# Sparse attention of a prompt: score masks added by VectorE, fewer score matmuls, three transpose banks; the kept-row copies moved to the first feed-forward

## What is computed

```
def masked_softmax(s, mask):
    s = jnp.where(mask, s, -jnp.inf)
    m = jnp.max(s, axis=-1, keepdims=True)
    m = jnp.where(jnp.isfinite(m), m, 0.0)
    p = jnp.exp(s - m)
    return p / jnp.maximum(jnp.sum(p, axis=-1, keepdims=True), 1e-30)
...
    p_cmp = masked_softmax(ein('bqhgd,bnhd->bqhgn', q, kc) * scale, mc)
    o_cmp = ein('bqhgn,bnhd->bqhgd', p_cmp, vc)
...
    o_sel = ein('bqhgk,bqhkd->bqhgd', masked_softmax(ein('bqhgd,bqhkd->bqhgk', q_rot, ks) * scale, ms), vs)
...
    o_win = ein('bqhgn,bnhd->bqhgd', masked_softmax(ein('bqhgd,bnhd->bqhgn', q_rot, kw) * scale, mw), vw)
    o = gates[..., 0:1] * o_cmp + gates[..., 1:2] * o_sel + gates[..., 2:3] * o_win
```

## Time and profile before

| | us |
|---|---|
| median of 3 runs | 5331.67 (5325.77 to 5340.48) |
| the profiled execution, its own time | 5327.34 |
| its span on the core | 5325.6 |
| PE busy in the span | 3931.5 (74%) |
| DVE, ACT, POOL busy | 1657.2, 977.1, 1442.9 |
| `ffn0`, first to last matmul tile | about 1795 to 2570 |
| `c_in`, first matmul to the last copy | 2635 to 2852 |
| prompt attention, loads included | about 3338 to 4100 |

### The profile page before, as it was taken

How to read it: one execution, slowest core, us unless ns; L and a number is a source line. 1 busy time by engine, 2 the same in 40 slices (tenths; PEclk the granted TensorE clock), 3 DMA queues, 4 the chain that set the end, 5 groups by cost and what they waited for, 6 DMA issues and landing times. The chain is left out here.

```text
span 5325.6 us, 63783 instructions
## 1 busy us (share of the span) xinstructions
PE 3931.5 (74%) x23500; PEld 3473.1 (65%) x23500; DVE 1657.2 (31%) x3084; ACT 977.1 (18%) x2173; POOL 1442.9 (27%) x1031
## 2 busy tenths in 40 slices
PE   3999044544533899999692567799997558999998
PEld 3999033434522899999682557456654228999998
DVE  3000422223425322223203121346664232322322
ACT  1000023310112201001100011345543122100102
POOL 3332400000001533333523000134443015333333
PEclk7999555555655999999796676689999669999999
DMA  3221521151134111111287311310100321111111
GB/s 110 101 86 60 179 84 55 48 210 49 59 95 135 38 44 47 45 44 42 83 298 239 71 56 39 61 25 13 25 1 21 102 82 40 44 48 44 42 50 53
DMA packets 364821, 395.59 MB, mean 74 GB/s; under 512 B 82945, under 2 KB 330467, under 8 KB 361111
## 3 DMA queue, kind: packets, MB, share of 16 engines
q1 hardware_dynamic: 321274, 263.06, 16.3%
q10 hardware_dynamic: 32076, 82.57, 4.8%
q0 software_dynamic: 11248, 46.95, 2.5%
HBM read 326.48 MB, written 133.75 MB: 86 GB/s over the span
## 5 line engine op out<-in xcount | busy, mean ns | idle before, releaser
L550 PE MATMUL ffn_ps<-ffn_x_hi,ffn_w_hi 128*128 128x384 f32 (+1 forms) x2112 | 688.0, 326 | 17.2 <-DVE ffn_x_lo L223 17.2
L550 PE MATMUL ffn_ps<-ffn_x_lo,ffn_w_hi 128*128 128x384 f32 (+1 forms) x2112 | 684.6, 324 | 0.0
L550 PE MATMUL ffn_ps<-ffn_x_hi,ffn_w_lo 128*128 128x384 f32 (+1 forms) x2112 | 683.5, 324 | 0.0
L2266 POOL TENSOR_TENSOR nsa_p_p<-nsa_p_p,nsa_p_w 128x63 f32<-128x63 f32 (+8 forms) x384 | 299.4, 807 | 863.7 <-DVE nsa_p_w L2222 852.4
L395 POOL TENSOR_TENSOR ffn_w_hi<-ffn_w,ffn_zero 128x1024 fp32r<-128x1024 f32 (+2 forms) x152 | 254.0, 1671 | 911.6 <-PE ffn_ps L550 903.5
L550 PEld LDWEIGHTS ffn_ps<-ffn_x_hi,ffn_w_hi 128*128 128x128 f32 x2112 | 398.9, 189 | 19.6 <-issue 19.6
L550 PEld LDWEIGHTS ffn_ps<-ffn_x_hi,ffn_w_lo 128*128 128x128 f32 x2112 | 399.0, 189 | 0.0
L550 PEld LDWEIGHTS ffn_ps<-ffn_x_lo,ffn_w_hi 128*128 128x128 f32 x2112 | 398.9, 189 | 0.0
L550 PE MATMUL ffn_ps<-ffn_h_hi,ffn_w_hi 128*128 128x384 f32 (+1 forms) x1056 | 344.1, 326 | 16.8 <-DVEq L618 16.8
L550 PE MATMUL ffn_ps<-ffn_h_lo,ffn_w_hi 128*128 128x384 f32 (+1 forms) x1056 | 342.7, 324 | 0.0
L550 PE MATMUL ffn_ps<-ffn_h_hi,ffn_w_lo 128*128 128x384 f32 (+1 forms) x1056 | 342.6, 324 | 0.0
(11 more groups left out here) (520 smaller groups left out, 7407.1 us busy)
## 6 DMA issues: line engine op xcount, KB each, us to landing
out<-in_cache_a_kv ACTq DMA_DIRECT2D x8, 4088.0 KB
ffn_w<-in_w_ffn_gate SPq DMA_DIRECT2D x44, 512.0 KB, 3.9
ffn_w<-in_w_ffn_up SPq DMA_DIRECT2D x44, 512.0 KB, 3.9
z_ab<-ab_in_o SPq DMA_DIRECT2D x90, 218.0 KB, 2.0
ab_in_w<-in_w_in_ab POOLq DMA_DIRECT2D x10, 1744.0 KB, 8.3
dil_s_kv<-in_cache_a_kv SPq DMA_DIRECT2D x16, 1024.0 KB, 33.5
cmp_pg<-in_cache_c_cmp_kv SPq DMA_DIRECT2D x128, 128.0 KB, 2.0
nsa_s_kv<-in_cache_c_sel_kv SPq DMA_DIRECT2D x128, 128.0 KB, 2.1
```

Of the source, the lines that this page charges most:

```text
L550: last = nc.tensor.matmul(bank(q)[:, 0:n], x[:, slot, k], y[:, k, c:c + n], start=(k == 0 and m == 0), stop=(k == kc - 1 and m == 2))
L2266: g.tensor_tensor(row[:, at:at + c], row[:, at:at + c], w[:, m, br:br + 1].to_broadcast([P, c]), ALU.mult)
```

## The change

In the prompt attention: the masks are no longer multiplied into the bank. PE writes the scores in one matmul per half (plus the compressed one), and DVE adds the masks in place, in the bank, ahead of the maxima, with a drain between. psP has three banks, one of them gained by dropping psF: `finish` now writes into the ring of psP. ACT copies two of three turned banks, DVE the third. Rounds are taken in pairs of groups: at an even group those of the next odd group too. The constants for the mask matmuls go. And `keep_rows` leaves the input projection: ACT of the first feed-forward starts two copies at each of the steps f = 0 to 15, between the tanhs and the copies of h.

```diff
-    rounds = lambda u, g: range(lead(u, g - 1) if g else (lead(u - 1, groups(u - 1) - 1) if u else 0), lead(u, g))
+    upto = lambda u, g: lead(u, min(g | 1, groups(u) - 1))
+    rounds = lambda u, g: range(upto(u, g - 1) if g else (upto(u - 1, groups(u - 1) - 1) if u else 0), upto(u, g))
+    last_first = lambda u: min(3, groups(u) - 1)
...
+    PB = 3
+    by_act = lambda t: t % 3 != 2
...
-        psS, psP = pb("psS", [P, 2, 1024]), pb("psP", [P, 2, EH, P])
-        psO, psF = pb("psO", [P, EH, P]), pb("psF", [P, 2, P])
+        psS, psP, psO = pb("psS", [P, 2, 1024]), pb("psP", [P, PB, EH, P]), pb("psO", [P, EH, P])
...
-                    mask(diag_bank, c1 - P, P, causalR[:])
-                    if comp and i >= WT:
-                        mask(0, c0, P, earlyR[:])
                     if comp:
-                        mask(bank, ca, DC, cmaskR[:, i])
...
-                    if early_block:
-                        part(0, c0, P, q_lo, keys(lo, 0, 1), False)
-                    if nb > na + 1:
-                        part(1, 512, (nb - na - 1) * P, q_up, keys(up, na, nb - 1), False)
...
+                    ends = {0: M(S[:, c0:512], q_lo, keys(lo, 0, na), start=True, stop=True)}
+                    if nb > 1:
+                        ends[1] = M(S[:, 512:c1], q_up, keys(up, na, nb), start=True, stop=True)
...
                 def finish(u):
+                    t = final_turn(u)
                     pe.wait_ge(o_copied, u + 1)
-                    if u:
-                        pe.wait_ge(f_copied, u)
+                    free_bank(t)
...
@@ def maxima(r) @@
+                    v.tensor_tensor(S[:, c1 - P:c1], S[:, c1 - P:c1], causal, ALU.add)
+                    if b:
+                        ca = comp_area(e)
+                        if i >= WT:
+                            v.tensor_tensor(S[:, c0:c0 + P], S[:, c0:c0 + P], early, ALU.add)
+                        v.tensor_tensor(S[:, ca:ca + NCMP_P], S[:, ca:ca + NCMP_P], cmask[:, i], ALU.add)
+                    v.drain()
                     v.reduce_max(mx[:, m, 1 + b:2 + b], S[:, c0:c1], AX.X)
...
@@ ffn_stream, ACT @@
                         for g, (c, n) in enumerate(GROUPS):
+                            if g == 0 and meanwhile is not None:
+                                meanwhile(act, f0 + f)
                             act.wait_ge(h_ready, NG * (f0 + f) + g + 1)
...
+        COPIES = 2
+
+        def keep_rows(eng, f):
+            for n in range(f * COPIES, (f + 1) * COPIES):
+                if n < DEC_B * len(keep):
+                    to, of, w = keep[n % len(keep)]
+                    b = n // len(keep)
                     eng.dma_start(to[b, 0:w - DEC_T], of[b, DEC_T:w]).then_inc(kept, 16)
...
-            feed_forward(0, res[:], ssq[:])
+            feed_forward(0, res[:], ssq[:], keep_rows)
...
-            mixer_in("c", res[:], ssq[:], k["gain10"], i["w_in_c"][0], z_c, N_C, 2, keep_rows)
+            mixer_in("c", res[:], ssq[:], k["gain10"], i["w_in_c"][0], z_c, N_C, 2)
```

More of the change, by code:

```diff
@@ L2087, in finish @@
                 def finish(u):
+                    t = final_turn(u)
                     pe.wait_ge(o_copied, u + 1)
-                    if u:
-                        pe.wait_ge(f_copied, u)
+                    free_bank(t)
                     for e in range(2):
-                        M(psF[e * DC:(e + 1) * DC], I2[:], ohalf[:, u % 2, e::2], start=True, stop=True).then_inc(final, 1)
+                        last = M(psP[e * DC:(e + 1) * DC, t % PB, 0:2], I2[:], ohalf[:, u % 2, e::2], start=True, stop=True)
+                        last.then_inc((turned_lo, turned)[e], 1)
                 pe.wait_ge(k_loaded, 32 * 2 * KVH)
@@ L2132, in copy_queries @@
                     eng.wait_ge(scored, 2 * 2 * EH * UN * (i - 1))
-                copy_turn(eng, copy, t, to, psP[:, t % 2])
+                copy_turn(eng, copy, t, to, psP[:, t % PB])
             def copy_group(eng, copy, u, g):
@@ L2226, in copy_out @@
                     if u >= 2:
-                        dve.wait_ge(final, 2 * (u - 1))
+                        dve.wait_ge(turned_lo, u - 1)
+                        dve.wait_ge(turned, final_turn(u - 2) + 1)
                     v.tensor_copy(ohalf[:, u % 2], psO[:]).then_inc(o_copied, 1)
-                v.tensor_copy(identR[:], ident)
-                v.tensor_copy(causalR[:], causal)
-                v.tensor_copy(earlyR[:], early)
-                v.memset(cmaskR[:].bitcast(F32), 0.0)
-                v.tensor_tensor(I2[:], ident[:, 0:DC], ident[:, DC:P], ALU.add)
-                v.drain()
-                v.tensor_copy(cmaskR[:, :, 0:NCMP_P], cmask)
-                v.drain().then_inc(consts, 1)
-                for t in range(1, KTURNS, 2):
-                    copy_keys(dve, v.tensor_copy, t)
-                for m in range(1, QTURNS, 2):
-                    copy_queries(dve, v.tensor_copy, 0, m, KTURNS + m)
+                v.tensor_tensor(I2[:], ident[:, 0:DC], ident[:, DC:P], ALU.add).then_inc(consts, 1)
+                for t in range(KTURNS):
+                    if not by_act(t):
+                        copy_keys(dve, v.tensor_copy, t)
+                for m in range(QTURNS):
+                    if not by_act(KTURNS + m):
+                        copy_queries(dve, v.tensor_copy, 0, m, KTURNS + m)
                 for u in range(UNITS):
@@ L2256, in _ @@
                             copy_out(u - 1)
+                        if u and g == last_first(u) and not by_act(final_turn(u - 1)):
+                            copy_final(dve, v.tensor_copy, u - 1)
                 copy_out(UNITS - 1)
+                if not by_act(final_turn(UNITS - 1)):
+                    copy_final(dve, v.tensor_copy, UNITS - 1)
             @block.gpsimd
```

123 lines of the change are left out of this document (56 added, 67 removed).

## The result

The changed kernel takes 5259.09 us (median of 4 runs, 5254.32 to 5263.35) against 5334.15 for the kernel before beside it: a ratio of 0.986, 95% interval 0.9843 to 0.9877. The forecast of 5228 was too low by 31 us; the range holds the time. The profiled execution has a span of 5258.9 us, 66.7 less than before.

What follows compares the result with a forecast made beforehand. Kept rows bound the projection's end, PE the first feed-forward; late attention was a loop of mostly PE work. Projection -33, feed-forward 0, attention -39 and -32 make -104: 5223 from 5327.3, 5228 from the median; range 5180 to 5300.

Steps and rivals of the forecast that it cites:

- DVE becomes the bound: Rival: in attention DVE's additions and chain set the pace, attention gains only 0 to -20, about 5289 us; chance 0.17.
- -71: Attention's forecast gain in us: -39 for blocks 4 to 7 and -32 for blocks 0 to 3.
- Copies out of the projection, -33: Input projection: without kept rows beside the stores, the last tile's wait goes, -33 us, bounds -34 and -17.
- Copies into the feed-forward, 0: First feed-forward: copies cost 0 us because the second weight slot covers late loads; bounds 0 and +24.
- PE sheds 0.76 per head: Attention, blocks 4 to 7: without mask matmuls PE saves 0.76 us per head, 3.0 per unit of four heads.
- What is not hidden is the last odd round: Attention, blocks 4 to 7: of DVE's additions only the last odd round's show, its maxima 0.8 us later per unit.
- Pairs left out of the price: Attention, blocks 4 to 7: the reordering by pairing rounds was given no price, its sign being open.
- the third bank at "near nothing": Attention: psP's third bank removes PE's waits for copies, near nothing now; up to 0.5 us per loop.
- A unit of 26.07 us: Late attention: two units start 26.07 us apart, of which PE's work is about 25.3.
- The first turns of block 7: Sign: 23.4 us apart if the forecast is right, still 25 if wrong.
- The rival with the clock: Rival: granted clock falls in late attention, at 0.75 adding 53 us there, 5368 us in all; chance 0.07.
- The rule on the pipe's drain: Attention: an operation waits for an empty pipe, so additions cost about 3 us more; set aside for measured rows.

Runs made afterwards that it cites:

- kept_only: The kernel before with only the copies of kept rows moved from the projection to the first feed-forward: 5304.0 us, ratio 0.9954 to the kernel before.
- pe_masks: The changed kernel with the masks multiplied into the bank by PE as before and DVE's additions gone: 5287.0 us, ratio 0.9927 to the kernel before.
- no_masks: The changed kernel without DVE's additions and the drain behind them, so masks are left out altogether: 5207.5 us, ratio 0.9778 to the kernel before.
- no_pair: The changed kernel with rounds issued group by group as before, not in pairs: 5288.2 us, ratio 0.992 to the kernel before.
- two_banks: The changed kernel with two turn banks instead of three: 5310.2 us, ratio 0.9955 to the kernel before.
- masks_alone: The kernel before with the copies moved and the masks given to DVE, nothing else of the attention changed: 5313.8 us, ratio 0.9963 to the kernel before.
- four_merged: The changed kernel with four one-bank score buffers in blocks 0 to 2 and one addition fewer in odd rounds: 5209.9 us, ratio 0.9765 to the kernel before.
- four_all: The changed kernel with four one-bank score buffers in blocks 0 to 2, one addition fewer in odd rounds, ACT copying all turned banks: 5200.1 us, ratio 0.9745.

## Why the prediction was right in direction and too large

The direction and the projection's part were forecast for the right reasons. That the range holds the time is in part its width: it was drawn to take in the rival "DVE becomes the bound" with 0 to -20 for the attention, and the measured -32 lies nearer to that than to -71.

- **Copies out of the projection, -33:** right, 30.7 from the first copy to the last, and 30.6 in kept_only. The release by PE and the stores' 2.0 us are as forecast.
- **Copies into the feed-forward, 0:** right to the microsecond in its mechanism. The load was put at 2112 landing for need at 2117; it landed at 2111.5 for 2116.04. The Trainium skill ("DMA: Bandwidth & Descriptors", section "Queues, rings and completion order") has the DMA engines alternate between queues; 14.2 us beside the copies against 3.8 alone agrees.
- **PE sheds 0.76 per head:** right in kind, a third too large in blocks 4 to 7. The forecast's 3.0 per unit there and 2.4 to 3.9 in the blocks before measure 2.0 (16 us in 8 units, twice) and 3.2 (48 us in 15 units, part of it clock: 0.82 with the masks on PE, 0.91 without): 80 us together by pe_masks against no_masks.
- **"What is not hidden is the last odd round", +0.8 per unit:** this is the step that failed. The additions cost 2.4 us per unit in blocks 0 to 3, 1.6 in blocks 4 and 5 and, as forecast, 0.8 in 6 and 7, 55 us in all. I set them beside DVE's load, 19 of 23.4 us, when the limit was latency: with two score buffers each round waits until the scores, additions, maxima and exponentials of the round before last are through. I had named this chain under the rival "DVE becomes the bound" and put it aside by DVE's idle share, which says nothing of it. DVE is not full after either (65 to 75%). In blocks 0 to 3 more than half of the cost is not the waiting itself but PE's matmuls at a lower granted clock, a path that the forecast had named for blocks 4 to 7 alone. Taken in turn, pairs, bank and copies with the masks still on PE make +3, -5 and -5 us (pe_masks against before), the masks off PE -48, -16 and -16, and the additions +36, +13 and +6.
- **Pairs left out of the price, the third bank at "near nothing":** wrong twice. Of the 50 us by which the changed kernel is ahead of kept_only, 32 go without pairs (no_pair), all without the third bank (two_banks), and 36 with the masks back on PE (pe_masks); the masks' move alone gains none (masks_alone). So the net gain needs all three together, and it can't be shared out among them. The bank without pairs may keep part of it: the stretches of no_pair are within 5 us of masks_alone, but its ratio is lower. That PE waited little for banks before spoke for the old order only: with two banks its waits for copies are 6, 6 and 7 us without pairs (masks_alone) and 17, 13 and 14 with them (two_banks).
- **A unit of 26.07 us:** it was a long one; the eight units of the last stretch average 24.8 before and 23.0 after. The first turns of block 7 were to come 23.4 us apart. They come 24.4 and 25.4 apart:

```profile
3942.61 1.09 PE L2045 MATMUL nsa_p_psP<-c_ident,nsa_p_p 128*128 128x128 f32 x8 [1.00 <-POOLq L2263]
...
3966.97 1.09 PE L2045 MATMUL nsa_p_psP<-c_ident,nsa_p_p 128*128 128x128 f32 x8 [0.56 <-POOLq L2263]
...
3992.36 0.88 PE L2045 MATMUL nsa_p_psP<-c_ident,nsa_p_p 128*128 128x128 f32 x6 [0.57 <-POOLq L2263]
```

- **The rival with the clock:** present in part. Blocks 4 to 7 stand at 0.96 and 0.99 instead of 1.00, and at 0.94 and 0.95 in no_pair. The 954 matmuls of blocks 4 and 5 keep PE busy for 174 us at 0.96 and for 166 at 1.00 (no_masks), so this is worth 8 us there.
- **The rule on the pipe's drain** (Trainium skill, "VectorE: DVE Perf Modes", section "The DRAIN you can't avoid"): the section adds that a next operation that is not held starts earlier, which the prediction left out (the advice on few operations stands in that page's "Rules for kernel authors"). An addition of 0.30 us at 3454.68 is followed by the next at 3454.88, so these neighbours do overlap, by 0.10 us. Whether the number of additions or their length counted is open (four_merged).

## What to carry to other kernels

Work moved from a busy engine to an idle one is paid in latency if it lands between a producer and the release of its buffer. Before comparing busy shares, look in the producer's order at what stands between filling a buffer and filling it again, and compare that with the buffer's turn around: here it was one other round, scored 0.63 us behind the first (3454.61), against 2.97. Averages hide this: a unit of block 1 takes 19.6 us for 8 rounds, 2.4 us a round, and two buffers with a turn around of 2.97 would keep that up if the rounds came evenly. Parts of a change can be worth little alone and much together, here the masks off PE, rounds in pairs and a third bank for what the pairs set free; undo each alone before crediting any. Where shapes are small, it can pay to spend banks on more buffers rather than on wider ones: four one-bank buffers in the first three blocks, with fewer matmuls, gave 36 us beyond the change.

## What the runs showed that I had not expected

Neither PE's busy share nor its idle time tells the granted clock. In the first stretch pe_masks keeps PE busy for 281 of 300 us and is granted 0.82, the changed kernel for 236 of 288 and 0.83, four_all for 204 of 237 and 0.96. What decides it stays open, though in blocks 0 to 3 it made more of the additions' cost than PE's idle time did. And with two wide buffers a second set of additions of the same length costs about as much as the first or more (35, 15, 12 against 36, 13, 6 us): hardly any slack took it up.
